# A short set-up phase, first weight tiles split one phase ahead, and residual additions bank by bank

## What is computed

```
x = x + 0.5 * swiglu(rms_norm(x, ffn1_norm), ffn1_w_gate, ffn1_w_up, ffn1_w_down)    # feed-forward 1
x = x + token_mixer(rms_norm(x, mix_norm), w_in, ..., w_out, rel_bias, 0)            # first mixer
x = x + 0.5 * swiglu(rms_norm(x, ffn2_norm), ffn2_w_gate, ffn2_w_up, ffn2_w_down)    # feed-forward 2
x = layer(x, ctx, c, c_ctx, p, False)                                                # second block

def swiglu(x, w_gate, w_up, w_down):
    return (silu(x @ w_gate) * (x @ w_up)) @ w_down
```

## Time and profile before

| | |
|---|---|
| median of 3 runs | 2274.76 us (2274.58 to 2277.65) |
| the profiled execution, its own time | 2273.07 us |
| its span, first to last instruction | 2271.2 us |
| PE busy | 1747.2 us, 77% |
| DVE, ACT, POOL busy | 826.3, 649.2, 230.5 us |
| mean granted TensorE clock | 0.883 |
| mean DMA rate over the span | 259 GB/s |

### The profile page before, as it was taken

One profiled execution on the slowest core, in us unless ns is written; L12 is line 12 of the kernel. 1 busy time (PEld: TensorE's weight loads), 2 busy tenths in 40 slices (PEclk: granted clock), 3 DMA queues, 4 the chain that ended last, 5 costly groups with the idle time before them and its releaser, 6 DMA issues. The chain is left out here.

```text
span 2271.2 us, 36447 instructions
## 1 busy us (share of the span) xinstructions
PE 1747.2 (77%) x15949; PEld 1176.4 (52%) x15949; DVE 826.3 (36%) x1185; ACT 649.2 (29%) x1051; POOL 230.5 (10%) x222
## 2 busy tenths in 40 slices
PE   6998997988999977897979976556565656655664
PEld 6997996876879866796769751111111111111111
DVE  4654435765665565676566640000000000000001
ACT  4333544564423355433443320000000000000001
POOL 0100003431131033101340000000000000000000
PEclk9999998999999988898789988787778788787888
DMA  6654652234955542153025569999999999999997
GB/s 200 201 186 147 188 176 75 89 112 158 302 168 187 164 129 77 58 172 117 4 76 184 201 270 424 428 428 428 428 428 428 428 428 427 428 428 428 427 428 308
DMA packets 181890, 588.39 MB, mean 259 GB/s; under 512 B 11355, under 2 KB 144150, under 8 KB 156902
## 3 DMA queue, kind: packets, MB, share of 16 engines
q1 hardware_dynamic: 180186, 585.10, 66.9%
q10 hardware_dynamic: 1548, 0.98, 0.2%
HBM read 584.88 MB, written 1.17 MB: 258 GB/s over the span
## 5 line engine op out<-in xcount | busy, mean ns | idle before, releaser
L193 DVE TENSOR_TENSOR split_lo<-ring,split_hi 128x2048 fp32r<-128x2048 f32 x127 | 295.8, 2331 | 198.5 <-ACT split_hi L186 197.8
L3569 PE MATMUL ps<-ex_ring,ex_xe 128*32 128x512 f32 x1440 | 228.6, 768 | 164.1 <-DMA ex_ring<-in_exp_w 164.1
L3650 DVE TENSOR_TENSOR ex_hid<-ps,ex_silu 128x512 f32<-128x512 f32 x16 | 11.1, 692 | 862.8 <-PE ps L3569 862.8
L221 PE MATMUL ps<-xt_hi,split_hi 128*128 128x256 f32 x984 | 283.9, 289 | 15.8 <-DVE xt_lo L402 7.3
L186 ACT CAST split_hi<-ring 128x2048 fp32r<-128x2048 f32 x127 | 240.2, 1896 | 176.2 <-PE ps L223 120.4
L222 PE MATMUL ps<-xt_lo,split_hi 128*128 128x256 f32 x984 | 278.9, 283 | 0.0
L223 PE MATMUL ps<-xt_hi,split_lo 128*128 128x256 f32 x984 | 278.7, 283 | 0.0
L3569 PEld LDWEIGHTS ps<-ex_ring,ex_xe 128*32 128x32 f32 x1440 | 44.5, 126 | 341.4 <-DMA ex_ring<-in_exp_w 250.1
L221 PEld LDWEIGHTS ps<-xt_hi,split_hi 128*128 128x128 f32 x984 | 188.1, 191 | 27.0 <-issue 20.5
L221 PE MATMUL ps<-split_hi,xt_hi 128*128 128x256 f32 (+1 forms) x560 | 176.6, 315 | 17.3 <-DVE split_lo L193 7.0
L222 PEld LDWEIGHTS ps<-xt_lo,split_hi 128*128 128x128 f32 x984 | 188.2, 191 | 1.2 <-issue 1.2
(11 more groups left out here) (761 smaller groups left out, 2811.0 us busy)
## 6 DMA issues: line engine op xcount, KB each, us to landing
ex_ring<-in_exp_w SPq DMA_DIRECT2D x133, 2048.0 KB, 46.1
ring<-in_exp_w SPq DMA_DIRECT2D x39, 2048.0 KB, 45.8
ring<-in_w_in SPq DMA_DIRECT2D x55, 1024.0 KB, 5.3
ex_late<-in_exp_w SPq DMA_DIRECT2D x18, 2048.0 KB, 45.9
ring<-in_ffn_w_gate SPq DMA_DIRECT2D x22, 1024.0 KB, 5.8
ring<-in_ffn_w_up SPq DMA_DIRECT2D x22, 1024.0 KB, 5.4
ring<-in_ffn_w_down SPq DMA_DIRECT2D x22, 1024.0 KB, 5.0
ring<-in_mod_w SPq DMA_DIRECT2D x16, 1024.0 KB, 5.7
```

The costliest lines, as they stand in the source:

```text
L193: eng.tensor_tensor(g.wlo[:, s % H, 0:n], g.ring[:, i % R, 0:n], g.whi[:, s % H, 0:n].bitcast(F32), ALU.subtract).then_inc(g.tiles_split, 1)
L221: nc.tensor.matmul(out, lhs[0], rhs[0], start=start, stop=False, skip_group_check=shared)
L3569: mm = mm_(ps[32 * q:32 * q + 32, 4 + u, :], xe[:, k], w[:, 512 * q:512 * q + 512], start=k == 0, stop=k == KC - 1)
L3650: v.tensor_tensor(hid[:], ps[:, 5, :], silu[:], ALU.mult).then_inc(S["hid"], 1)
```

## The change

Five edits.

1. **Set-up.** It loads only the identity and the eight rows of `ffn1_norm` (both from ScalarE's queue), x and the first four weight tiles (SyncE's queue), transposes the eight rows and copies them. Everything else moves into the new class `Vectors`, a side object of feed-forward 1: its 35 small DMAs are issued by SyncE at the head of that phase, the transposes stand ahead of tile k = 8, the bias product and lambda's sums at k = 10, ScalarE's exponential at k = 11, lambda's end and the store of the bias by distance at k = 12.
2. **Entry of feed-forward 1.** The first tile is split behind two quarters (`split_after` = 2) instead of ahead of all.
3. **First tiles split ahead.** Feed-forward 1 splits the first tile of `w_in` (`ahead` = 1), `mixer_out` the first tile of feed-forward 2 (`out0 + 4`); the entries of the mixer and of feed-forward 2 don't split their first tile (`SPLIT_AHEAD`, a number that q never reaches).
4. **Last down tile of both feed-forwards.** The loops run bank by bank, each bank signals on its own, and VectorE adds each when it is done.
5. **Last `w_out` product.** The second token half of `out0 + 3` runs bank by bank, with the same kind of signal for the first of the two.

```diff
@@ Entry
     def act(self, act):
-        split_hi(nc, g, act, self.first)
         for q in range(4):
+            if q == self.split_after:
+                split_hi(nc, g, act, self.first)
             act.wait_ge(S["turned"], q + 1)
...
     def dve(self, dve):
-        split_lo(nc, g, dve, self.first)
         for q in range(4):
+            if q == self.split_after:
+                split_lo(nc, g, dve, self.first)
             dve.wait_ge(S["xt_hi"], q + 1)
@@ setup_phase
         @block.scalar
         def _(act):
-            put_rows(act, VEC_A, VEC_A_ROWS, ROW_A, 0)
...
+            act.dma_start(g.ident[:], I["k_ident"]).then_inc(S["ident"], 16)
+            act.dma_start(gain[:], I["ffn1_norm"][0].rearrange("(r n) -> r n", n=P)).then_inc(S["gain"], 16)
 
         @block.sync
         def _(sp):
-            sp.dma_start(g.ident[:], I["k_ident"]).then_inc(S["ident"], 16)
-            put_rows(sp, VEC_B, VEC_B_ROWS, ROW_B, 1)
             sp.dma_start(g.x[:], I["x"].rearrange("b (t p) d -> p (b t) d", p=P)).then_inc(S["x"], 16)
-            load_tiles(g, sp, 2)
             load_tiles(g, sp, R)
-            sp.dma_start(g.causal[:], I["k_causal"]).then_inc(g.bias_stored, 16)
             sp.wait_ge(S["x"], 16)
-            sp.wait_ge(S["dbias"], 1)
-            sp.dma_start(g.bias_dram, dbias[:]).then_inc(g.bias_stored, 16)
@@ class Vectors (the side object of feed-forward 1)
+    COLS, BIAS, LAM = 8, 10, 12
+    ahead = 1
...
+    def load(self, sp, k):
+        if k == self.LAM:
+            sp.wait_ge(self.S["dbias"], 1)
+            sp.dma_start(self.g.bias_dram, self.g.dist_bias[:]).then_inc(self.g.bias_stored, 16)
...
+    def act(self, act, k):
+        if k == self.BIAS + 1:
+            act.wait_ge(self.S["lamsum"], 1)
+            self.nc.scalar.activation(self.lamv[:, 258:260], self.lamv[:, 256:258], ACT.Exp).then_inc(self.S["lamexp"], 1)
@@ ffn_phase
-        tiles = list(range(first, down0 + pairs + (AHEAD if side else 0)))
+        tiles = list(range(first, down0 + pairs + (side.ahead if side else 0)))
...
+                if m == pairs - 1:
+                    for q, (t, n) in enumerate(Entry.order):
+                        for c in range(2):
+                            mm = product3(nc, ps[:, 4 + 2 * t + n, :], [x[:, c, P * t:P * t + P] for x in hidden(m)],
+                                          [x[:, c, 512 * n:512 * n + 512] for x in w], False, c == 1)
+                        mm.then_inc(g.split_used if q == 3 else S["summed"], 1)
+                    continue
...
-            wait_used(g, dve, down0 + pairs - 1)
-            for t in range(TT):
-                for n in range(2):
-                    xs = g.x[:, t, 512 * n:512 * n + 512]
-                    nc.vector.scalar_tensor_tensor(xs, ps[:, 4 + 2 * t + n, :], 0.5, xs, ALU.mult, ALU.add)
+            for q, (t, n) in enumerate(Entry.order):
+                if q == 3:
+                    wait_used(g, dve, down0 + pairs - 1)
+                else:
+                    dve.wait_ge(S["summed"], q + 1)
+                xs = g.x[:, t, 512 * n:512 * n + 512]
+                nc.vector.scalar_tensor_tensor(xs, ps[:, 4 + 2 * t + n, :], 0.5, xs, ALU.mult, ALU.add)
@@ mixer_out
+            split_hi(nc, g, act, out0 + 4)
...
+            split_lo(nc, g, dve, out0 + 4)
+            dve.wait_ge(S["first_summed"], 4)
+            v.tensor_tensor(g.x[:, 0], summed(4, 0), g.x[:, 0], ALU.add)
+            for n in range(2):
+                if n:
                     wait_used(g, dve, out0 + 3)
                 else:
-                    dve.wait_ge(S["first_summed"], 4)
-                xs = g.x[:, t]
-                v.tensor_tensor(xs, summed(4, t), xs, ALU.add)
+                    dve.wait_ge(S["half_summed"], 1)
+                xs = g.x[:, 1, 512 * n:512 * n + 512]
+                v.tensor_tensor(xs, ps[:, 6 + n, :], xs, ALU.add)
```

155 lines of the change are left out of this document (100 added, 55 removed).

## The result

The changed kernel takes 2253.18 us, the median of 4 runs (2250.3 to 2255.77), against 2274.67 (2273.83 to 2277.65) for the kernel before on the same chip: a ratio of 0.9914, interval 0.9901 to 0.9926. The medians differ by 21.5, 15.8 and 18.3 us, 18.5 on average. The profiled execution took 2254.35 us, 18.7 less than that of before.

What follows compares the result with a forecast made beforehand. Ahead of the experts, whose weight stream is DMA-bound, TensorE was taken to set the pace and lose time at joints. Terms 6.4 + 4.05 + 2.9 + 1.85 = 15.2 us off 2273.07, plus 1.7 for a median: 2259.5 us, range 2254.5 to 2264.5.

Steps and rivals of the forecast that it cites:

- Set-up: Start of the kernel: x asked for at 0.74 us, fourth tile released at 9.3, first transpose at 9.9 (9.6 to 10.6).
- The rival of a set-up that ends a tile later: Set-up: release comes one tile later (3.4 us), first transpose at 13.3 us, total 2263; chance 0.10.
- Entry of feed-forward 1: First transpose to first product takes 7.7 us, 1.3 longer than before; first product at 17.6 us, 7.6 earlier.
- Vectors: Small transposes and bias product moved into feed-forward 1 cost TensorE 1.2 us (0.9 to 2.4); other engines' work is hidden.
- Feed-forward 1 into the mixer: Three additions beside the last products save 1.86 us, the shorter mixer entry 2.2; together 4.05 (3.7 to 4.3).
- the clock stays up: Rival for the mixer and feed-forward 2 entries: shorter idling avoids the 1.2 GHz level, 2 to 3 us more, 2257; chance 0.17.
- Mixer into feed-forward 2: Last addition half as long saves 0.6 us, the entry without its split 2.3; together 2.9 (2.4 to 3.0).
- Feed-forward 2 into the context phase: Additions beside feed-forward 2's last products save 1.86 us again, entered in the sum as 1.85.
- The sum up to the context phase: All savings from set-up to the context phase's start: 6.4 + 4.05 + 2.9 + 1.85 = 15.2 us.
- Behind the context phase: From the context phase's start to the end: no further gain, forecast 0 us; experts' stage as long as before.
- Small loads starving the ring: Rival in feed-forward 1: 35 issues delay the fifth tile past 29 us; at 1.0 us each total 2278; chance 0.03.
- The rival that the experts absorb the gain: Experts' weight stream begins at a time of its own, so earlier savings don't count: 2274.8 us; chance 0.05.

Runs made afterwards that it cites:

- later_4: The changed kernel with four small loads that nothing reads ahead of x in SyncE's queue; 2254.89 us.
- later_8: The changed kernel with eight small loads that nothing reads ahead of x in SyncE's queue; 2258.94 us.
- two_tiles: The changed kernel with only two weight tiles loaded in the set-up, the other two at the head of feed-forward 1's loads; 2249.32 us, run again 2251.7.
- two_warm: The changed kernel with two weight tiles in the set-up, plus a tiny ScalarE activation there to load its table; 2249.33 us, ratio 0.9908 to before.
- splits_only: The kernel before with only the first tiles of the mixer and feed-forward 2 split one phase ahead; 2262.36 us, ratio 0.9967.
- tails_only: The kernel before with only the last down tiles, the last w_out product and their additions bank by bank; 2269.47 us, ratio 0.9986.
- setup_only: The changed kernel without the splits ahead and the bank-by-bank tails, leaving set-up, vectors and feed-forward 1's entry; 2267.16 us, ratio 0.9978 to before.
- loads_twice: The changed kernel with 35 more small loads that nothing reads ahead of the fifth weight tile; 2257.43 us, ratio 0.9948 to before.

## Why the prediction was right, and what it mis-sized

**Set-up: right.** Release forecast 9.3, measured 9.40; first transpose 9.9 and 9.97; first product 17.6 and 17.56. The rival of a set-up that ends a tile later did not come: later_4 and later_8 show that the release follows x's place in the queue, by 0.94/1.48 = 0.64 and 2.40/2.83 = 0.85 us for each microsecond. The prediction took the distance from x's issue to the release from the kernel before (9.2 us, less 0.7) and gave no mechanism for it. The release follows the landing of the first tile by 0.01 to 0.09 us in all ten profiles with the new set-up; with the old one the two lie within 0.5 us of each other in four, so that the landing alone lets the issue go is likely and not shown. two_tiles shows what is late next: with two tiles out of the set-up the transposes start at 7.30, 0.8 us behind the transpose of the gain's rows (6.49), which waits for their transfer. (The bounds of 4.3 to 7.5 us for set-up and entry together don't follow from the bounds of the terms: 6.9 - 2.4 = 4.5 and 7.9 - 0.9 = 7.0 do.)

**Entry of feed-forward 1: right, for one reason less than stated.** 7.59 us against 7.7. The table load was charged 0.4 us net; two_warm shows 0.12, since the first quarter isn't ready much before. The prediction also saw that the entry gets longer by the order of edit 2; that this order may be a loss of about 1 us it didn't ask.

**Vectors: inside the bounds, but sized too small.** Feed-forward 1 of the changed kernel has the vectors' products between its own (timeline, TensorE; the two bias products overlap):

```profile
65.53 0.26 PE L505 MATMUL ps<-ident,vec_rows 114*128 114x114 f32 x1
65.72 0.40 PE L507 MATMUL ps<-ident,wide_rows 12*128 12x12 f32 x2
66.06 0.33 PE L508 MATMUL ps<-ident,vec_rows 124*128 124x124 f32 x1
77.68 0.81 PE L512 MATMUL ps<-buckets 32*20 32x383 f32 x2
```

From first to last product that phase took 191.13 to 191.34 us in three profiles, 189.71 and 190.25 before: 0.9 to 1.6 more, forecast 1.2. But this holds the slow stretch at the phase's start as well, which was shorter in the changed kernel (7.50 to 7.70 us for the first 48 products, against 7.96 and 8.50). From the 49th product on the phase takes 183.61 to 183.64 us in the three and 181.75 in the two: the vectors cost 1.9 us. The forecast halved the set-up's pace and left out what the products around them lose: where the first group of transposes stands, two neighbouring products are 0.73 us apart, and around the bias products 0.95, in place of 0.12; the rest is spread over the phase.

**Feed-forward 1 into the mixer: the term right, a part beside it missing.** 4.12 us against 4.05. But the mixer's entry also lost its stretch at the 1.2 GHz level, another 1.5 to 2.0 us. I had this as the rival *the clock stays up* with a chance of 0.17, and argued from the 4.54 us wait ahead of feed-forward 2 that some stretch would remain. For the mixer it never did, in ten profiles; splits_only shows that the wait between transposes and product decides, and tails_only that the idling at the tail doesn't. That is the step of the prediction that failed: the slow stretch of the entry was counted as staying, although the wait ahead of it was cut from 2.9 us to 2.2. In the first pair of profiles it was hidden: the first 48 products gave 7.26 - 5.73 = 1.5 us, but the gain in the mixer from product to product was only 0.34, since the kernel after had a stretch at a clock of 0.50 from 506.1 to 509.5 us that the profile of before doesn't have; the averages of the table over mixer entry to feed-forward 2 entry (335.2 before, 331.3 after, so 3.8 less, where 2.2 + 0.6 = 2.8 was forecast) show a full microsecond of it.

**Mixer into feed-forward 2: right.** 2.86 against 2.9, and the moved split cost nothing (0.51 us of idling ahead of it). The rival was half true here: five executions of ten without the slow stretch, which is worth 7.27 - 5.76 = 1.5 us.

**Feed-forward 2 into the context phase: sized too large.** 1.37 against 1.85, in all nine profiles with the whole change (TensorE idles 1.51 us in each). The term was copied from feed-forward 1. But this phase has a side object, which splits tiles of the next phase ahead, and in the kernel before the last such split ended 1.29 us ahead of the additions. With the additions moved forward it stands in their way: they run as an unbroken four behind it and end 1.14 us behind the last product, where one addition of 0.69 us was forecast.

**The sum up to the context phase: in part luck.** 14.9 against 15.2 hides larger misses. The vectors took 0.7 us more than forecast and the last joint gave 0.5 less; the slow stretches behind the first products of feed-forward 1 and of the mixer gave 0.5 and 1.5 us that weren't forecast, and the rest of the mixer, which has one more stretch at a clock of 0.50, took 1.2 back.

**Behind the context phase: a term put at nothing.** The forecast was made against one profiled execution as if the pace of the untouched work were the same in every execution. Between context phase and router TensorE's busy time was 4.4 us shorter at the same idle time, and no edit changes an instruction there; the medians' gains of 21.5, 15.8 and 18.3 us may hold such luck as well. Set-up, joints and the mixer's clock make 15.2 + 1.7 = 16.9 us, or 17.7 with half of feed-forward 2's stretch. The average of the three gains, 18.5, is near this, with an interval of some 3 us on each.

**Small loads starving the ring: didn't happen** (the fifth tile is issued at 24.07, forecast 23.2, and TensorE is busy for all of 24 to 200 us), **and its sizing was off by two errors that in part cancel.** I had TensorE wait from an issue at 29 us on, one microsecond for each. With the issue at 36.09, 7.1 us behind that limit, it waited 3.23, so the wait begins at an issue near 33 us. But the clock falls after the wait, which the rival left out, and the two together cost 5.7, where the rival would have had 7.1.

**The rival that the experts absorb the gain: didn't come,** as forecast. Router to end takes 948.8 to 949.9 us in all five profiles.

**Open.** What makes this stretch differ by 5 us over 535 us between executions wasn't found, nor whether it leans to the changed kernel: with all of the change in it the stretch from context phase to router took 533.9 to 538.0 us in nine profiles, in before (two) and setup_only 538.7 to 539.5, and in splits_only and tails_only 536.6 and 537.0. Whether the order of edit 2 costs time in the changed kernel is open too.

## What to carry to other kernels

Follow each joint from the last product to the next first one, also for what an earlier edit has put there: work that is split ahead for the next phase can stand in the way of additions that were moved forward, as in feed-forward 2. Then count each wait of TensorE twice: once as idling and once for the clock behind it, which in this kernel's mixer stayed up after a wait of 2.2 us and fell after 2.9. Where a queue ends a phase, look which of its transfers the next phase truly needs: two of four tiles sufficed here for an earlier first product. Don't compare a forecast with a single profile below 0.2%, since stretches without a changed instruction move by 5 us.

## What the runs showed of the hardware beyond that

- The same 16 transposes take 1.94 us after 1.1 or 1.64 us of TensorE idling and 2.84 to 3.60 after 2.9.
- Full clock has two paces. The mixer's tiles take 5.600 us each in some executions and 5.654 in others, both at a granted clock of 1.00, in one kernel (the changed one: 5.654 twice, 5.600 once). Over 19 tiles that is 1.0 us. In the ten profiles with the short entries, the five at 5.654 are the five with the slow stretch behind feed-forward 2's entry.
- A DMA's issue is held by large transfers ahead of it: the third tile's issue took 4.14 us and the fourth's 2.86 in the changed kernel, the small loads behind them 0.3 us each (in loads_twice 0.35). The third tile's issue ends 0.13 to 0.20 us after x has landed, the fourth's 0.01 to 0.09 us after the first tile has.
- A wait of 3.23 us for a late tile was followed by nearly 6 us at the 1.2 GHz level, 5.7 - 3.2 = 2.5 us more lost.
- Where DMA is the bound, the clock didn't matter: the experts took 949.3 us with 169 us lost to the lower level and 949.9 with 198.
